# Feed-forward by quarters: order of VectorE's sums and low parts, waits between GpSimd's splits, and two state outputs issued later

## The reference, cut to what matters

```python
for layer in range(DEPTH):                       # 2
    h = _rmsnorm(x, norm_mix[layer])
    mix, state = mixer(h, ...)                   # attention and mLSTM in layer 0, GLA in layer 1
    x = x + mix @ w_out[layer]                   # 1024 x 1024
    h = _rmsnorm(x, norm_ffn[layer])
    x = x + jnp.square(jax.nn.relu(h @ w_ff1[layer])) @ w_ff2[layer]   # 1024 -> 4096 -> 1024
y = _rmsnorm(x, norm_final)
```

## Time and profile before

| | |
|---|---|
| median of 3 runs | 3145.7 us (3143.62 to 3148.36) |
| the profiled execution | 3147.87 us, span of its instructions 3146.1 us |
| busy: PE, PEld, DVE, ACT, POOL | 93%, 86%, 46%, 29%, 35% of the span |
| mean granted TensorE clock | 0.969 |
| chain that ended last: PE, DVE, ACT, issue | 82%, 8%, 3%, 4% |
| line 463 (hidden rows and projections), 7344 matmuls | 1289.3 us busy |
| line 616 (products by quarters), 2688 matmuls | 338.2 + 241.9 us and the ninths |
| PE line 616 idle until VectorE's sums, line 917 | 44.6 us, 14 times |

### The profile page before, as it was taken

One profiled execution on the slowest core, in us unless ns is written; L12 is line 12 of the kernel. 1 busy time (PEld: TensorE's weight loads), 2 busy tenths in 40 slices (PEclk: granted clock), 3 DMA queues, 4 the chain that ended last, 5 costly groups with the idle time before them and its releaser, 6 DMA issues.

```text
span 3146.1 us, 42736 instructions
## 1 busy us (share of the span) xinstructions
PE 2931.5 (93%) x17570; PEld 2706.7 (86%) x17570; DVE 1453.2 (46%) x1967; ACT 924.2 (29%) x1406; POOL 1091.1 (35%) x616
## 2 busy tenths in 40 slices
PE   5999988888999999999999999897899999999998
PEld 5999977687989888898888999886898898888987
DVE  4500246564354556545532410295336545565453
ACT  4411346352322222222223302352232222222222
POOL 1122345132144434434412132473214434444331
PEclk8999999999999999999999999999999999999999
DMA  3112230233001111011102121203301011100111
GB/s 128 41 42 71 84 107 1 81 99 136 27 27 40 54 53 37 16 53 53 60 28 105 60 86 56 104 1 101 132 29 40 16 52 53 53 27 27 53 60 61
DMA packets 120322, 185.39 MB, mean 59 GB/s; under 512 B 11333, under 2 KB 84257, under 8 KB 119428
## 3 DMA queue, kind: packets, MB, share of 16 engines
q1 hardware_dynamic: 108784, 139.97, 13.7%
q0 software_dynamic: 11280, 43.50, 3.9%
q10 hardware_dynamic: 132, 0.13, 0.0%
HBM read 150.34 MB, written 33.20 MB: 58 GB/s over the span
## 4 chain that ended last, share of the span: by engine, by line
PE 82%; DVE 8%; issue 4%; ACT 3%; POOL 1%; DMA 1%; DVEq 0%; POOLq 0%; ACTq 0%; SPq 0%
PE ps L463 41%; PE ps L616 17%; PE ps L473 13%; PE ps L695 3%; DVE units L917 1%; DVE glrow_r L912 1%; PE ps L1697 1%; DVE small L2573 1%; PE ps L1678 1%; PE ps L412 1%; DMA units<-x_prompt 1%; DVE units L905 1%; PE ps L2003 1%; ACT units L753 1%; ACT units_r L759 0%
## 5 line engine op out<-in xcount | busy, mean ns | idle before, releaser
L463 PE MATMUL ps<-units_r,split 128*128 128x384 f32 x7344 | 1289.3, 336 | 10.8 <-DVEq L276 10.8
L463 PEld LDWEIGHTS ps<-units_r,split 128*128 128x128 f32 x7344 | 1284.7, 189 | 15.8 <-issue 14.5
L473 PE MATMUL ps<-split,units_r 128*128 128x256 f32 x3456 | 427.2, 286 | 25.0 <-DVE units_r L538 23.4
L473 PEld LDWEIGHTS ps<-split,units_r 128*128 128x128 f32 x3456 | 422.1, 194 | 26.5 <-issue 19.4
L854 POOL TENSOR_TENSOR split<-raw,split 128x1024 fp32r<-128x1024 f32 x98 | 264.7, 2701 | 514.6 <-ACT split L756 514.6
L256 POOL TENSOR_TENSOR split<-raw,split 128x2048 fp32r<-128x2048 f32 x44 | 203.5, 4626 | 605.9 <-ACT split L251 605.9
L616 PE MATMUL ps<-split,units_r 128*128 128x512 f32 x1344 | 338.2, 412 | 44.6 <-DVE units L917 44.6
L616 PEld LDWEIGHTS ps<-split,units_r 128*128 128x128 f32 x1344 | 268.7, 201 | 109.7 <-DVE units L917 50.5
L917 DVE TENSOR_TENSOR units<-units,ps 128x512 f32<-128x512 f32 x434 | 287.7, 684 | 163.0 <-PE ps L616 162.3
L905 DVE TENSOR_TENSOR units<-units 128x1152 f32<-128x1152 f32 x56 | 106.7, 1906 | 451.0 <-ACT units L753 451.0
L616 PE MATMUL ps<-split,spare_r 128*128 128x512 f32 x1008 | 241.9, 395 | 0.0
(11 more groups left out here) (398 smaller groups left out, 3270.1 us busy)
## 6 DMA issues: line engine op xcount, KB each, us to landing
raw<-w_ff SPq DMA_DIRECT2D x64, 1024.0 KB, 5.4
raw<-w_in_even SPq DMA_DIRECT2D x14, 1024.0 KB, 5.3
raw<-w_in_odd SPq DMA_DIRECT2D x12, 1024.0 KB, 5.4
raw<-w_out SPq DMA_DIRECT2D x8, 1024.0 KB, 8.3
units<-x_prompt SPq DMA_DIRECT2D x4, 1536.0 KB, 9.7
stream<-units POOLq DMA_DIRECT2D x1, 4608.0 KB, 14.7
park_gv<-spare POOLq DMA_DIRECT2D x36, 128.0 KB, 2.1
units<-park_gv SPq DMA_DIRECT2D x3, 1536.0 KB, 10.7
```

The source lines that it names most:

```text
L463: last = pe.matmul(ps[:, bank + n, 0:GN], weights(slab, a, k, c0, P), h[b][:, k, n * GN:(n + 1) * GN], start=(k == 0 and q == 0), stop=(k ...
L473: last = pe.matmul(out, h[b][:, k, n * P:(n + 1) * P], weights(slab, a, k, 0, COLS), start=(k == 0 and q == 0), stop=(k == KC - 1 and q == 2))
```

## The change

VectorE: the second ninth's low part comes before a1's, and the reading of the first six sums comes before p21 and p11. TensorE: the ninth waits for `left(4)` alone, a1's products for `left(5)`, and the counts of `right` follow GpSimd's new order. GpSimd: b12's split (slot 3) and right_sum's (slot 0) come before `b21 - right_sum`; it waits for `ff_sq` 7 before right_sum's split and for `ff_lo` 6 before that difference. ScalarE: the ninth's high part before a1's, a0's (with its wait `squared(7)`) behind two right high parts, and `made(10)` for `made(8)`. In `last_block`, the second half's `begin` goes to its first matmul group. At the start of the first output projection the puts of states 2 and 3 are issued after the split of slab 1 and not before the stage begins.

```diff
@@ -500,9 +500,11 @@
                 hi_of(act, base + m)
             norm_tiles_act(act, 2 * layer + 1, own, w_add, 4 * NT * layer + 3 * NT)
 
-        def out_pool(pool, layer):
+        def out_pool(pool, layer, between):
             for m in range(0 if layer else 1, 5):
                 lo_of(pool, (OUT0, OUT1)[layer] + m)
+                if m == 1:
+                    between()
 
         def out_pe(pe, layer, between):
             h = part(0), part(4)
@@ -648,17 +650,18 @@
                 right(4)
                 product(4, ninth(0), 1, True, True, True).then_inc(ff_y, 1)
                 right(7)
+                left(4)
+                product(5, ninth(1), 2, False, True, True).then_inc(ff_y, 1)
                 left(5)
-                product(5, ninth(1), 2, False, True, True).then_inc(ff_y, 1)
                 for n in SUMS_FIRST:
                     if n >= 2:
                         taken(3 + n)
                     product(Y_BANK[n], tile(a1, n), 2, True, True, False).then_inc(ff_y, 1)
-                right(9)
+                right(8)
                 for n in SUMS_FIRST:
                     taken(7 + n)
                     product(Y_BANK[n], tile(a2, n), 3, True, True, n == 0).then_inc(ff_y, 1)
-                right(10)
+                right(9)
                 left(6)
                 for n in SUMS_FIRST:
                     taken(1 + n)
@@ -696,7 +699,7 @@
                                             weights(base + 2 + half, a, k, 0, 512, 512),
                                             start=(k == 0 and q == 0), stop=(k == HC - 1 and q == 2))
 
-                            begin(one, n == 0 and q == 0 and k == (0, HC - 1)[half])
+                            begin(one, n == 0 and q == 0 and k == 0)
                     return one
 
 
@@ -778,20 +781,20 @@
                 freed(3)
                 right_high(2, right_raw(base, 1, 0))
                 squared(5)
+                left_high(left_ninth[:, 0, 2:4], plain[:, 2:4, SEQ:T])
                 left_high(a1[:, 0], quarter(plain, 0, 1))
-                left_high(left_ninth[:, 0, 2:4], plain[:, 2:4, SEQ:T])
                 made(5)
                 right_high(3, right_raw(base, 0, 1))
-                squared(7)
                 freed(4)
-                left_high(a0[:, 0], quarter(plain, 0, 0))
                 made(6)
                 right_high(0, right_sum)
                 freed(5)
                 right_high(1, right_raw(base, 0, 0))
+                squared(7)
+                left_high(a0[:, 0], quarter(plain, 0, 0))
                 freed(6)
                 left_high(a1[:, 0], quarter(plain, 1, 0))
-                made(8)
+                made(10)
                 right_high(2, right_raw(base, 1, 0))
                 freed(7)
                 left_high(a2[:, 0], quarter(plain, 1, 1))
@@ -839,6 +842,7 @@
 
         def mlp_pool(pool, layer, base, gain):
             highs, splits = slabs_done(base, HI), slabs_done(base, LO)
+            squares, lows = counted(layer, 8, HC), counted(layer, 9, HC)
 
             def summed_block(blk):
                 def high(count):
@@ -871,12 +875,14 @@
                 minus(right_sum, b22, b11)
                 high(4)
                 right_low(2, b21)
-                made(7)
-                minus(b21, b21, right_sum)
                 high(5)
                 right_low(3, b12)
+                pool.wait_ge(ff_sq, blk * 8 + (squares + 7))
                 high(6)
                 right_low(0, right_sum)
+                made(7)
+                pool.wait_ge(ff_lo, blk * 9 + (lows + 6))
+                minus(b21, b21, right_sum)
                 high(7)
                 right_low(1, b11)
                 high(8)
@@ -927,15 +933,15 @@
                 low(3, a2[:, 1], s3, a2[:, 0])
                 square(2)
                 square(3)
-                low(4, a1[:, 1], p12, a1[:, 0])
-                low(5, left_ninth[:, 1, 2:4], plain[:, 2:4, SEQ:T], left_ninth[:, 0, 2:4])
-                dve.tensor_tensor(p21, p21, p22, ALU.add).then_inc(ff_sq, 1)
-                squared(6)
-                dve.tensor_tensor(p11, p21, p11, ALU.subtract).then_inc(ff_sq, 1)
+                low(4, left_ninth[:, 1, 2:4], plain[:, 2:4, SEQ:T], left_ninth[:, 0, 2:4])
+                low(5, a1[:, 1], p12, a1[:, 0])
                 for n in SUMS_FIRST:
                     add(1 + n, n, 0, X_BANK[n])
                 add(5, PT, 1, 4)
                 add(6, PT, 0, 5)
+                dve.tensor_tensor(p21, p21, p22, ALU.add).then_inc(ff_sq, 1)
+                squared(6)
+                dve.tensor_tensor(p11, p21, p11, ALU.subtract).then_inc(ff_sq, 1)
                 dve.wait_ge(ff_add, blk * READS + (sums + 4))
                 for n in SUMS_FIRST:
                     add(7 + n, n, 0, Y_BANK[n])
@@ -1458,13 +1464,11 @@
             pool.wait_ge(c_out, 16 * 2)
             pool.wait_ge(out_done, outs[0])
             leave(pool, pool_stage)
-            put(state_to(2), CRAW[2])
-            put(state_to(3), CRAW[3])
 
 
             enter(pool, S_OUT0)
             gain(1)
-            out_pool(pool, 0)
+            out_pool(pool, 0, lambda: (put(state_to(2), CRAW[2]), put(state_to(3), CRAW[3])))
             leave(pool, pool_stage)
             enter(pool, S_FF0)
             mlp_pool(pool, 0, MLP0, lambda: gain(2))
@@ -1560,7 +1564,7 @@
 
             enter(pool, S_OUT1)
             gain(3)
-            out_pool(pool, 1)
+            out_pool(pool, 1, lambda: None)
             leave(pool, pool_stage)
             enter(pool, S_FF1)
             mlp_pool(pool, 1, MLP1, lambda: gain(4))
```

## The result

The changed kernel takes 3088.76 us, median of four runs (3088.04 to 3091.26), beside 3144.66 us (3141.78 to 3148.36) of the kernel before on the same chip: ratio 0.9823, 95% interval 0.9806 to 0.9840, which is 50 to 61 us less. The forecast was 3089 (3060 to 3110). The spans of the two profiled executions are 3146.1 and 3086.2 us, 59.9 apart.

What follows compares the result with a forecast made beforehand. TensorE was taken to bound the kernel, losing about 5.5 us a feed-forward block to late sums, as VectorE and GpSimd exclude each other. Gains 51 - 4 + 5.5 + 3.5 = 56 us gave 3089 us, range 3060 to 3110.

Steps and rivals of the forecast that it cites:

- The new wait: In each feed-forward block, TensorE waits about 1.75 us for low 7 and sum 15, before a1's products on the X banks.
- the one before the a2 products: In each block, sum 7 is done about when TensorE wants it for the a2 products; 0.1 us booked.
- The period: Time of one feed-forward block on the chain: about 96.1 us in place of 99.73.
- rival (b): In the block, a1's low part goes before b12's split, so the new wait is 0.9 us: 3072 us, chance 0.20.
- Rival (a): In the block, the port goes to VectorE between GpSimd's splits, so no new wait: 3061 us, chance 0.17.
- (c): In the block, the new wait lowers the clock each time: 3109 us, chance 0.12.
- (d): GpSimd keeps the port through b11, b21 and b22 before a1's low part, wait 4.1 us: slower, 3165 us, chance 0.03.
- (e): No gain, as the sums are bound by something not seen: 3137 to 3146 us, chance 0.03.
- The loop: The 14 feed-forward blocks lose 1.85 us each in place of 5.5: 3.65 x 14 = 51 us gained.
- The clock's part behind the new wait: In the blocks, slow matmuls after the new wait cost between nothing and 23 us; 4 us taken.
- The puts: At the first output projection, puts after slab 1's split end the third tile's wait: 5.5 us gained (3 to 6.7).
- The last block: In layer 0's last block, the earlier signal lets `scaled` end sooner: 3.5 us gained (1.9 to 3.9).

Runs made afterwards that it cites:

- e6: Changed kernel with one more GpSimd wait: b12's split starts only when a1's low part (the fifth) is done; 3074.0 us, ratio 0.9763.
- e1: Changed kernel with one more GpSimd wait: b21's split starts only when a1's low part (the seventh) is done; 3062.3 us, ratio 0.9731.
- e2: Changed kernel with only VectorE's order altered: a1's low part, then sums 15 to 18, then p12; 3062.3 us, ratio 0.9733.
- e3: Changed kernel without GpSimd's two new waits (ff_sq 7 and ff_lo 6), all else as changed; 3132.1 us, ratio 0.9952.
- e4: Kernel before with one edit alone: VectorE reads sums 1 to 6 ahead of p21 and p11; 3148.7 us, ratio 1.000.
- e7: Changed kernel with p21 and p11 ahead of sums 1 to 6 again, GpSimd's new order and pauses kept; 3097.2 us, ratio 0.9839.
- e5: Changed kernel with the two edits outside the loop undone (puts and the last block's begin); 3101.0 us, ratio 0.9843.

## Why the prediction was right

*The mechanism.* The steps of the block came as worked out, to about 0.2 us. The new wait was put at "about 1.75" and measured 1.77; the one before the a2 products at 0.1 and the 24 + 24 matmuls there show it (48 in 11.20 in place of 11.05, with a restart's slower first interval in it). The period was put at 96.1 and is 96.16. That GpSimd goes first where both ask (rival (b) otherwise) is in the rows, and e6 priced the alternative: 3074.0 where (b) said 3072. Rival (a) had 3061, and e1, which takes its condition by force, gave 3062.3. Rivals (c), (d) and (e) did not occur: after the wait of 1.77 us no block of the 14 had slow matmuls, and GpSimd never kept the port for a second split while VectorE asked. That lost turns made the new wait is shown by e1 and e2: a pause took a1's low part from 3.42 to 1.21 us, a change of order put it ahead of p12 so that one lost turn (2.55) stood before sum 15 in place of two (2.56 and 3.42), and both took the same 26 us off. That an engine waits for the whole of the other's instruction, and that the two don't share bandwidth, e1 and e2 alone don't show, but the rows do: in the changed kernel's blocks 84 VectorE instructions of 1024 elements with two inputs in SBUF took over 1.45 us, issued from 1.4 to 2.4 us before the end of a GpSimd row, and every one ended 1.08 us after that row, about what such an instruction takes alone; in the kernel before it was all 70 (1.08 or 1.09).

*The sizes.* The loop was put at 51 us and gave 49.6 in the spans. The clock's part behind the new wait, 4 us, was nothing. (Its example was read a little high: 72 matmuls at the full level take 12.71 us behind the narrow ones, in the rows of before at 1745.84 with a granted clock of 1.00, and not the 12.49 taken from hidden rows, so the slow ones cost 1.5 us there.) The puts were put at 5.5 and gave 6.5: the 4.4 of waiting, and nearly all that the slow matmuls had cost. The last block was put at 3.5 and gave 3.6. So the forecast of 56 should have been 60 by its own terms; the spans differ by 59.9, the medians by 55.9, since the profiled execution of before was 3.2 us above the median of its four others (which scatter by 6.6 us) and that of the changed kernel 0.7 below its own. That 3089.0 stands beside 3088.8 is thus partly luck, of about 4 us.

*What the prediction didn't have.* It priced the sums' new place and GpSimd's pauses as one. e3, e4 and e7 part them: sums first alone brings nothing a block (e4), everything but the pauses 0.6 us (e3), everything but sums first 2.9 (e7), all of it 3.6. Read from the rows of before alone, I thought afterwards that the sums' place would do most of it, and was wrong (e4): a lost turn is not a constant, it depends on where the other engine stands when the instruction is issued, and a shift of 2 us ahead changes which instruction loses one.

What stays open: the two edits outside the loop were undone together; each one's share is read from the trace and has no run of its own. In the loop, ScalarE's new order, the order of GpSimd's splits and the ninth's low part first were not undone one by one, so what each gives beside the pauses is not shown.

## What to carry to other kernels

When an instruction with two inputs in SBUF is three times as long on VectorE in one stretch as in another, look at GpSimd's row that ends shortly before it does (1.1 us here, for 1024 elements), and count the turns lost ahead of the point for which TensorE waits. An engine with time to spare can buy those turns back: let it wait until the short chain of the other has passed (three semaphore waits took 33 us off here), and put instructions that don't contend, or that nobody waits for, where turns are lost anyway. Such edits have to be worked out along the whole block, since one that frees the first wait can pile up lost turns at the next (e4).

## What the runs showed of the hardware

Who gets the port next, with both engines queued, went strictly by turns in every block looked at: VectorE's p12 and low part each behind one split of 2.4 us and ending 1.08 us after it, GpSimd's split behind each of them. The Trainium skill (SBUF — State Buffer, section Who interferes with whom) says that issue order decides who blocks; b12's split, issued 0.04 us before a1's low part, agrees.

TensorE's waits of 3.2 to 3.3 us in a stream of matmuls were followed by matmuls at the lower clock level (1.2 GHz) in every block of before (36 in 9.92 us in the one of the earlier trace rows), and by half-clock matmuls in e3 and e4 too; waits of 0.9, 1.5 and 1.77 us never were, the last in 14 blocks of 14. In the first half of the slow stretch of the earlier trace rows the granted clock was 0.51 (1127.12 to 1130.50), after it 1.00. A wait between these went both ways: TensorE idle for 1.94 us before the transposes of layer 0's last block had slow matmuls behind it in the kernel before (12 in 4.57 us) and none in e5 (12 in 3.02 us). The six narrow matmuls over 2.13 us, four times in each trace, had the lower clock level behind them twice before and once after (14.24 us for 72 in place of 12.71).

The second of the two puts of 512 KB from GpSimd's queue had its row only when the first had landed: the two stand right behind each other in the changed kernel, with rows at 734.59 and 742.70, and the first landed at 742.36; in the kernel before their rows are at 726.72 and 736.28, and the first landed at 735.97. The queue stood for 8.1 and 9.6 us, and in the kernel before the split of slab 1 stood behind it. That it is the landing that frees the queue is read from these times and has no run of its own; the load of the norm's weights behind the second put (row at 737.17) was not held so.
